# A fused two-block model on one core: the second half of every w2 piece's rest is computed by GpSimd instead of VectorE

## What is computed

```python
def run_block(args):
    tok, g, e = args
    xb = h2[tok]
    y = (jax.nn.silu(xb @ w1[e]) * (xb @ w3[e])) @ w2[e]
    return y * g[:, None]
```

## Time and profile before

| what | value |
| --- | --- |
| median of 3 runs | 2029.89 us (2028.04 to 2037.18) |
| profiled execution, its own time | 2034.99 us |
| span of the profiled instructions | 2033.2 us |
| mean granted TensorE clock | 0.957 of full speed |
| PE busy | 93% of the span |
| DVE busy | 69% |
| ACT busy | 54% |
| GpSimd busy | 5% |
| experts' stage of layer 0, of layer 1 | about 250 to 563 us, 705 to 1018 us |

### The profile page before, as it was taken

How to read it: one execution, slowest core, us unless ns; L and a number is a source line. 1 busy time by engine, 2 the same in 40 slices (tenths; PEclk the granted TensorE clock), 3 DMA queues, 4 the chain that set the end, 5 groups by cost and what they waited for, 6 DMA issues and landing times.

```text
span 2033.2 us, 27015 instructions
## 1 busy us (share of the span) xinstructions
PE 1895.7 (93%) x11125; PEld 1619.2 (80%) x11125; DVE 1393.8 (69%) x1740; ACT 1095.2 (54%) x1419; POOL 107.2 (5%) x113
## 2 busy tenths in 40 slices
PE   4958899999979899999989999899999999989998
PEld 2935678888866678888789987789999998769997
DVE  2687488888876488888865556565566555656655
ACT  3433377777757377777744446454445445545433
POOL 0460010100000010100000000000000000000000
PEclk9978799999999799999999999899999999979999
DMA  9546579899959389999945555145555555424551
GB/s 365 199 152 253 216 279 342 313 336 344 338 209 323 124 299 324 327 338 326 353 143 186 193 189 173 62 146 187 194 198 168 192 200 193 137 81 148 198 194 53
DMA packets 209323, 457.25 MB, mean 225 GB/s; under 512 B 8848, under 2 KB 20776, under 8 KB 209192
## 3 DMA queue, kind: packets, MB, share of 16 engines
q1 hardware_dynamic: 204800, 450.99, 63.7%
q10 hardware_dynamic: 4392, 4.44, 0.7%
HBM read 454.35 MB, written 1.05 MB: 224 GB/s over the span
## 4 chain that ended last, share of the span: by engine, by line
PE 85%; DVE 9%; ACT 3%; DMA 1%; issue 1%; POOL 0%; SPq 0%; ACTq 0%; DVEq 0%; POOLq 0%
PE bank L299 82%; DVE arena L1242 2%; DVE rest L635 2%; PE bank L1958 2%; DVE arena L1234 1%; DMA raw<-in_mod_w 1%; PE bank L2226 1%; DMA raw<-in_od_out_w 1%; ACT arena L756 0%; ACT round L618 0%; DVE xres L1234 0%; DVE small L1234 0%; DVE small L1866 0%; ACT hTh L788 0%; DVE hTl L1234 0%
## 5 line engine op out<-in xcount | busy, mean ns | idle before, releaser
L635 DVE TENSOR_TENSOR rest<-raw,round 128x1024 fp32r<-128x1024 f32 (+1 forms) x760 | 892.1, 1222 | 259.4 <-ACT round L618 259.3
L618 ACT ACTIVATE round<-raw 128x1024 fp32r<-128x1024 f32 (+1 forms) x760 | 758.6, 1050 | 387.7 <-PE bank L299 382.5
L299 PE MATMUL bank<-hTh,round 128*128 128x256 f32 x1600 | 447.2, 279 | 16.2 <-DVE hTl L1234 12.8
L299 PE MATMUL bank<-hTl,round 128*128 128x256 f32 x1600 | 445.0, 278 | 0.0
L299 PE MATMUL bank<-hTh,rest 128*128 128x256 f32 x1600 | 444.9, 278 | 0.0
L299 PEld LDWEIGHTS bank<-hTh,round 128*128 128x128 f32 x1600 | 302.2, 189 | 22.5 <-issue 19.3
L299 PEld LDWEIGHTS bank<-hTl,round 128*128 128x128 f32 x1600 | 303.5, 190 | 1.0 <-issue 0.2
L299 PEld LDWEIGHTS bank<-hTh,rest 128*128 128x128 f32 x1600 | 302.0, 189 | 0.0
L299 PE MATMUL bank<-round,hTh 128*128 128x512 f32 x464 | 187.2, 403 | 6.8 <-DVE hTl L1234 3.1
L299 PE MATMUL bank<-round,hTl 128*128 128x512 f32 x464 | 183.6, 396 | 0.0
L299 PE MATMUL bank<-rest,hTh 128*128 128x512 f32 x464 | 182.7, 394 | 0.0
(11 more groups left out here) (223 smaller groups left out, 2306.6 us busy)
## 6 DMA issues: line engine op xcount, KB each, us to landing
raw<-in_ex_w SPq DMA_DIRECT2D x192, 1024.0 KB, 5.5
raw<-in_mod_w SPq DMA_DIRECT2D x48, 1024.0 KB, 6.9
raw<-in_ffn_w_gate SPq DMA_DIRECT2D x44, 1024.0 KB, 5.1
raw<-in_ffn_w_up SPq DMA_DIRECT2D x44, 1024.0 KB, 5.0
raw<-in_ffn_w_down SPq DMA_DIRECT2D x44, 1024.0 KB, 4.8
raw<-in_w_in SPq DMA_DIRECT2D x20, 1024.0 KB, 5.0
raw<-in_ev_in_w SPq DMA_DIRECT2D x10, 1024.0 KB, 13.8
raw<-in_od_in_w SPq DMA_DIRECT2D x8, 1024.0 KB, 5.8
```

The source lines that it names most:

```text
L299: return e.matmul(o, l, r, start=start, stop=stop, skip_group_check=True)
L618: e.activation(hi[:, h], raw[:, h], ACT.Copy).then_inc(S("hi"), 1)
L635: e.tensor_tensor(lo[:, h], raw[:, h], hi[:, h].bitcast(F32), ALU.subtract).then_inc(S("lo"), 1)
```

## The change

For the pieces of w2 of the experts (two a w2, 32 a layer, 64 in all) DVE subtracts the first half alone. GpSimd subtracts the second half. It waits until ACT has rounded the second half, and signals on a semaphore `lo_pool` of its own. PE waits for both engines before it takes a w2 piece. The count of `lo` is adapted (`lo_before`: two for each piece before, less one for each w2 piece). The one-hot tiles of groups 2 and 3 are now built after the halves of the pairs 0 and 2. To free a semaphore for `lo_pool`, the one-shot signal `odd_lam` shares another's counter. No other instruction changes.

```diff
@@ class Weights
+        self.pool_half = [self.plan[i][0][0] == "ex_w2" for i in self.split]
+        self.lo_before = [2 * m - sum(self.pool_half[:m]) for m in range(len(self.split) + 1)]
@@ dve_split
                 if j in W.nth:
                     dve_half(e, j, 0)
-                    dve_half(e, j, 1)
+                    if not W.pool_half[W.nth[j]]:
+                        dve_half(e, j, 1)
@@ pool_program
+            def second_half(j):
+                m, raw, hi, lo = piece(j)
+                half = raw.shape[1] // 2
+                e.wait_ge(S("hi"), 2 * m + 2)
+                e.tensor_tensor(lo[:, half:], raw[:, half:], hi[:, half:].bitcast(F32), ALU.subtract).then_inc(S("lo_pool"), 1)
+
             def moe(l):
-                for q in range(1, NQ):
-                    one_hot(l, q)
+                one_hot(l, 1)
+                for p in range(NP):
+                    for ex in PAIRS[p]:
+                        for r in (0, 256):
+                            second_half(W.where["ex_w2", (l, ex), r, 0])
+                    if p in (0, 2):
+                        one_hot(l, p // 2 + 2)
@@ pe_program, second(i)
-                e.wait_ge(S("lo"), 2 * W.nth[i] + 2)
+                e.wait_ge(S("lo"), W.lo_before[W.nth[i]] + 2)
@@ pe_program, take
-                    e.wait_ge(S("lo"), 2 * W.nth[i] + (2 if whole else 1))
+                    m = W.nth[i]
+                    if W.pool_half[m]:
+                        e.wait_ge(S("lo_pool"), sum(W.pool_half[:m + 1]))
+                    e.wait_ge(S("lo"), W.lo_before[m] + (2 if whole and not W.pool_half[m] else 1))
```

More of the change, by code:

```diff
@@ L213 @@
     "even_act": {"even_sig": 2, "even_q": 2, "even_k": 2, "even_sd0": 1, "even_qk0": 2, "even_sd1": 1, "even_v": 2,
-                 "even_qk1": 2, "even_ln": 2, "even_w": 6, "even_oh": 2, "even_usq": 1, "even_usd": 1, "even_uh": 1},
+                 "even_qk1": 2, "even_ln": 2, "even_w": 6, "even_oh": 2, "even_usq": 1, "even_usd": 1, "even_uh": 1, "odd_lam": 1},
     "even_dve": {"even_u": 2, "even_ss0": 1, "even_qn0": 1, "even_ss1": 1, "even_qn1": 1, "even_L": 6, "even_d": 6,
@@ L1616, in chain @@
                     own.see()
-                e.wait_ge(S("odd_lam"), 1)
+                e.wait_ge(*V("odd_lam", 1))
                 chain(ts(N8(1), N8(0), 2.0, None, ALU.add))
```

## The result

The changed kernel takes **2058.32 us** (median of 4 runs, 2048.61 to 2062.10) against 2031.95 us before (median of 4 runs, 2028.04 to 2037.18): a ratio of 1.0106, 95% interval 1.0073 to 1.0138. It is slower by about 1%. The forecast of 2057 us holds, but two of its sizes were off in opposite directions, and only the trace shows it: 2057 us is in part luck.

The account below looks back on a forecast made before the run. PE bounds the experts' stages. Lateness of 6 x 1.8 + 1.1 + 1.7 = 13.6 us a layer gives 27 us for two, 2062 us for the profiled execution; with the median 5 us lower, 2057 us, range 2030 to 2085.

Parts of the forecast that it names:

- What bounds the kernel: Inside the experts' stages PE is busy for 240.00 of 240 us and waits for nobody; a faster DVE brings nothing.
- term 1: Removing 64 halves of 1.18 us from DVE frees 75 us of busy time, worth nothing on the path inside the stage.
- The alternation: On w2 halves, DVE and GpSimd take turns by whole instructions: 1.18 + 2.4 = 3.58 us against PE's 2.75 a piece.
- side by side after all: Rival, chance 0.14: in the experts' stages GpSimd holds DVE under 1.95 us or not at all; time 2030 us.
- R: Time from the start of GpSimd's w2 half to DVE's release; taken as 2.4 us, bounds 1.9 and 2.55.
- Faster: Rival, chance 0.02: DVE's relief shortens an end of a stage; more than 10 us hardly to be had.
- dear conversion: Rival, chance 0.10: GpSimd's halves are slow because they write the rounded format, 4.8 us each; time 2200 us.
- the page's price: Rival, chance 0.06: same mechanism at a smaller price for GpSimd's half, R = 2.15, 5.7 us a layer, 2041 us.
- term 2: GpSimd's added halves, about 2.5 us each, make a group's fourth w2 piece 1.8 us late for PE (4R - 7.8).
- term 6: What else moves (DVE's later next piece, one-hot tiles, loads, extra wait) costs nothing; at most 20 us if cover were short.
- term 3: Pairs 1 to 6 repeat the group's lateness; in pair 7 the last w2 piece is 1.1 us late (4R - 8.5).
- term 4: At a layer's end the last activation split comes 1.7 us later, all of it on the path (3R - 5.6).

Follow-up runs that it names:

- e1: Against the changed kernel, GpSimd's w2 halves were left out and PE used the first half's rest twice: 2033.44 us, ratio 1.0000 to the kernel before.
- e2: Against the changed kernel, DVE's first halves of w2 pieces were left out and PE waited for GpSimd's alone: 2037.09 us, ratio 1.0030 to the kernel before.
- e5: Against the changed kernel, GpSimd also took the second halves of the w1 and w3 pieces: 2100.07 us in one run.
- e3: Against the changed kernel, GpSimd took second halves of only two w2 pieces of four, DVE the others whole: 2036.05 us, ratio 1.0021 to the kernel before.
- e9: The changed kernel unchanged, run and profiled again: 2050.89 us over six runs, ratio 1.0096 to the kernel before.
- e4: Against the changed kernel, GpSimd took the last quarter of each w2 piece and DVE the rest: 2036.45 us, ratio 1.0015 to the kernel before.

## Why the prediction was right, and where its sizes were not

**What bounds the kernel** stood as told. With DVE 25 us lighter in 240 (e1), PE's turn stayed at 38.19 us to the hundredth: no gain, term 1 at 0.

**The alternation** stood too: the 2.41 us that GpSimd takes alone (e2) and the 1.18 of DVE are harmless apart, and only together do they cost. The rival *side by side after all* falls with DVE's halves of 2.80 and 2.97 us; R is above its threshold of 1.95 by 0.23 us only (by 0.33 with the deadline found below, which puts the threshold at 1.85). What it is that the two engines share no run isolates: the runs show that two instructions with both operands in SBUF take turns. *Faster* falls with e1, the *dear conversion* with e2.

**The size of R was wrong.** The step that failed is the choice of 2.4 (bounds 1.9 to 2.55) under "what GpSimd's half costs". It measured 2.18, outside the forecast's own 2.25 to 2.6. Two things went into the 2.4. The duration was nearly right: 2.5 forecast, 2.41 to 2.50 when GpSimd neither waits nor is waited for. But 0.1 us was subtracted to get R, as read at a GpSimd instruction that had not waited before it ran. In a group GpSimd's instruction is already given out while DVE works, and from handover to end it takes 2.27 us, 0.14 less than the 2.41 alone; a part of it must pass in the wait, which part no run shows. With the 0.09 us between DVE's release (363.14) and GpSimd's end (363.23), R is 0.23 us less than the duration alone, not 0.1. The 256-column rows, where GpSimd did wait, had the same in them. The earlier trace rows is a sum of two rests; the second one by itself is

```profile
86.30 1.63 DVE L635 TENSOR_TENSOR rest<-raw,round 128x1024 fp32r<-128x1024 f32 x1
```

and the first ends at 84.62 + 1.76 = 86.38. GpSimd's instruction ends at 85.26 + 1.59 = 86.85, 0.47 us after that handover, where it takes 0.61 alone. The second rest ends at 87.93, so it was let go at 86.75, and GpSimd held it for 0.37 us: 0.24 less than the duration alone, as the 0.23 at 1024 columns. The prediction's 0.47 was the mean over both rests, and it scaled the hold by four. Scaling the duration and taking the fixed part off, 4 x 0.61 - 0.24 = 2.2, would have been the size. (The instructions of the earlier trace rows that read a PSUM bank are multiplications by the gate, not subtractions as the prediction has it, and only the second lies beside GpSimd's. Nothing hangs on that.)

The Trainium skill, GPSIMD Engine Reference, section 3.1, states 4497 ns for an addition of 2048 float32 columns on GpSimd; half of it, 2.25 us for 1024 columns, is an estimate. For the instruction alone e2's 2.41 us is 7% above that estimate, so the trace does not quite agree. For the alternation the rival *the page's price* (R = 2.15, chance 0.06) was nearer to 2.18 than the forecast's 2.4, but by two errors that cancel: a duration 0.16 us too low and 0.1 taken off instead of 0.23. The Trainium skill, SBUF — State Buffer, "Who interferes with whom", says that a DVE instruction with two SBUF inputs contends with a GpSimd instruction that reads SBUF, and calls the lock on the ports that the two share exclusive. The traces agree: 1.77 to 2.97 us for DVE's 1.18 in the group above, and turns that grow only when both engines have halves of a group (e1, e2).

**PE's deadline was taken 0.4 us too late.** By the prediction's formula R = 2.18 gives 3R - 6.2 = 0.3 us of lateness at C and 4R - 7.8 = 0.9 at D, so 0.9 a turn. Measured are 0.60 at C, another 0.60 at D and some 0.05 at B in pair 3, and 1.27 a turn on average. The further 0.60 at D is the formula's; C is late by 0.3 us more. The deadlines had been read from ACT's rounds. ACT's timeline after shows what such a round marks, now that PE's pieces no longer join:

```profile
373.13 2.01 ACT L620 ACTIVATE round<-raw 128x1024 fp32r<-128x1024 f32 x2 [1.35 <-PE bank L301]
```

The round starts 0.10 us after C's last product ends (372.64 + 0.39 = 373.03), and 0.21 before D's first one begins at 373.34. So it marks the end of the old piece, not the start of the new one; the signal `used` stands on the old piece's last product. Before, PE had begun the new piece by then. Its lines around C's start, products and weight load:

```profile
372.02 0.39 PE L299 MATMUL bank<-round,catTl 128*128 128x512 f32 x1
372.25 0.39 PE L299 MATMUL bank<-round,catTh 128*128 128x512 f32 x1
...
372.03 0.19 PEld L299 LDWEIGHTS bank<-round,catTh 128*128 128x128 f32 x1
```

C's first product starts at 372.25, not at 372.43, and its weight load at 372.03, with B's last product. This load takes an activation and needs nothing of the weight piece. But PE's wait for the piece (`take`) stands ahead of the load in its list, and after the change the load does wait (0.75 us of idle time above). The true deadline is thus the start of the old piece's last product, 0.4 us ahead of the one assumed. That makes 0.9 + 0.4 = 1.3 us a turn, against 1.27 measured.

The terms, forecast against measured:

```
                                        forecast    measured
R, us                                   2.4         2.18
a turn (term 2), us                     1.8         1.27 (1.14 to 1.40)
six turns of a layer                    10.8        7.6, 7.65
pair 7 and the end of a layer (3, 4)    2.8         1.2, 1.6
follow-ups (term 6)                     0           0
experts' stages, both layers (5)        27          18
```

With R = 2.18 term 3 is 0.2 and term 4 0.9 us, and the prediction's 31R - 61 is 6.6 a layer. The earlier deadline adds 0.4 in each of six turns and in pair 7: 9.4 a layer, 18.8 us in all against 18.0 measured. Term 4 can be read by itself at the end of layer 0 after, DVE's timeline:

```profile
555.19 1.59 DVE L637 TENSOR_TENSOR rest<-raw,round 128x1024 fp32r<-128x1024 f32 x1 [0.25 <-ACT round L620]
557.51 6.03 DVE L637 TENSOR_TENSOR rest<-raw,round 128x1024 fp32r<-128x1024 f32 x4 [0.74 <-ACT round L620]
563.46 1.27 DVE L1248 TENSOR_TENSOR catTl<-bank,catTh 128x512 fp32r<-128x512 f32 x2
```

From DVE's start on the last w2 piece (555.19) to the activation split (563.46) it is 8.27 us, where it was 552.50 to 559.84, 7.34: 0.93 later, as 3R - 5.6 has it. The four halves that follow the last w2 piece take 6.03 us instead of 4.7, since GpSimd's last half holds the first of them. PE waits 2.17 us for the split where it waited 1.54. With 0.6 us for D of pair 7 that is 1.5 us, and layer 1 shows 1.6. Layer 0 shows 1.2 because it was slower before: from PE's first product behind the split to the gated output it took 1.16 us (560.67 to 561.83), in layer 1 before and in layer 0 after 0.81. Why is open.

**Follow-ups at nothing** stood: the turn's 1.27 us is the sum of the late pieces of the group (0.05 + 0.60 + 0.60), and the pieces of w1 and w3 add nothing to it. With their second halves on GpSimd too (e5) that cover is gone, and the turns are 40.4 to 44.9 us. The one-hot tiles of later groups, which now stand behind four halves, cost nothing, nor did the extra wait (e3 has both, at a turn of 38.19).

**The time.** 27 us was forecast over the profile's 2034.99, less 5 for the median. The experts' stages gave 18, and the six runs of e9 differ from their median before by 19 us, 2050.9 in all. The first four runs differ by 26, of which the profiled one has 5.7 us in untouched stages. So that 2057 lies 1 us from the first result is luck: the working was too dear by half of what was found in the stages (27 for 18), and other differences filled the gap. A small part stays open: e2 and e3, whose turns and stages are those of before, have medians 4 to 5 us above it (intervals 1.0012 to 1.0048 and 1.0003 to 1.0039), while e1 has 1.0000. Whether such a part outside the experts' stages belongs to the change no run decides.

**The signs to look for** that the prediction named: GpSimd's halves of 3.6 us were 3.38; DVE's of up to 3.5 were 1.77 to 2.97 for B, C and D, and 3.42 for the piece behind them; a turn of 40 us was 39.3 to 39.6; PE's waits for GpSimd stand in 14 groups as forecast, 13 waits a layer (two in each of six groups, one in pair 7's), only in the last two pieces of a group, and equal, not growing, because once PE is late each piece adds the same 0.6.

## What to carry to other kernels

Before work is moved to an idle engine, ask in that stage's windows and waits whether the engine that is relieved holds anybody up, and whether the two engines can run at the same time at all; a pair that alternates costs the sum of both, and that sum (here 3.35 us) must stay below the consumer's step (2.75 us) or within the margin of a group. A margin lasts for a number of pieces: two of four were free, the third cost 0.7 us a turn and the fourth 0.6 more. Read a holding time from an instruction that had to wait, as it will in the new kernel, and an operand's deadline from the first instruction behind the wait for it in the consumer's list, here a weight load that starts with the product before, not from the first product.

## What the runs showed of the hardware

- GpSimd's subtraction of 1024 float32 columns with both operands in SBUF takes 2.41 us when DVE's halves of the same pieces are left out (e2, 64 times within 25 ns), 2.50 as the shortest in the changed kernel, and 2.25 to 2.27 from the handover when it has been waiting (B, C and D of pair 3). It holds DVE's two-operand instruction for 2.18 of that. A quarter of a piece holds it for 1.1 (e4).
- A wait of 0.32 us in the list of PE's waits cost 0.5 us between products and 0.6 us in the group's time.
- The granted clock was 1.00 in all windows of the experts' stages, also where PE was idle for 3.4 us in 240 (0.99 in e5, where it was idle for 11). So no part of the loss there is the clock's.
- In the second block the same program had one profile in which most 256-column products stood 117 to 119 ns apart and one (e9) in which most stood 113 to 114 ns apart, at a granted clock of 1.00 and 0.99 in the window 1040 to 1240 us; both spacings occur in either. Over the last stretch that is 10.7 us. Its cause was not looked for.
